# Gathering split around the first down products, columns ahead of weights, the eleventh place one matrix later

## The reference, cut to what matters

```
def run_block(args):
    xb, e = args
    hid = jax.nn.silu(xb @ w_gate[e]) * (xb @ w_up[e])
    return hid @ w_down[e]

ys = lax.map(run_block, (xs, blk_expert)).reshape(n_slots, D)
out = jnp.zeros((T + 1, D), jnp.float32).at[slot_tok].add(
    ys.astype(jnp.float32) * slot_gate[:, None])[:T]
```

## Time and profile before

| what | value |
|---|---|
| median of 3 runs | 941.4 us (941.03 to 943.34) |
| profiled execution, own time | 941.0 us |
| its span | 938.9 us |
| TensorE busy | 908.8 us, 97% |
| bytes moved by DMA | 286.12 MB, mean 305 GB/s |

### The profile page before, as it was taken

How to read it: one execution, slowest core, us unless ns; L and a number is a source line. 1 busy time by engine, 2 the same in 40 slices (tenths; PEclk the granted TensorE clock), 3 DMA queues, 4 the chain that set the end, 5 groups by cost and what they waited for, 6 DMA issues and landing times.

```text
span 938.9 us, 13252 instructions
## 1 busy us (share of the span) xinstructions
PE 908.8 (97%) x5218; PEld 537.0 (57%) x5218; DVE 277.9 (30%) x738; ACT 209.6 (22%) x500; POOL 198.7 (21%) x329
## 2 busy tenths in 40 slices
PE   7999999999999999999988999999999999999996
PEld 5788687544434444344433434488756558688544
DVE  2499824310101101011001011234135346250334
ACT  3365624211101111001101001132215511011640
POOL 0188400111111111111101111031003202013221
PEclk9999999999999999999999999999999999999999
DMA  9999975899999999999999999993300942202001
GB/s 349 428 425 419 405 297 203 347 384 431 428 427 429 427 428 424 429 427 428 428 427 429 427 422 425 427 414 140 156 2 19 427 171 114 89 14 77 1 1 45
DMA packets 24682, 286.12 MB, mean 305 GB/s; under 512 B 2738, under 2 KB 3506, under 8 KB 5426
## 3 DMA queue, kind: packets, MB, share of 16 engines
q1 hardware_dynamic: 23904, 283.99, 72.9%
q10 hardware_dynamic: 722, 1.33, 0.4%
HBM read 284.26 MB, written 1.05 MB: 304 GB/s over the span
## 4 chain that ended last, share of the span: by engine, by line
PE 74%; DMA 16%; DVE 6%; SPq 2%; issue 1%; POOL 0%; ACT 0%; POOLq 0%; DVEq 0%
PE bank L1032 18%; PE bank L1296 17%; DMA arena<-in_w_expert_up 10%; PE bank L1313 8%; PE bank L1517 5%; DVE bank L1772 5%; PE bank L1323 4%; DMA arena<-in_w_expert_down 3%; PE bank L1464 3%; DMA arena<-in_w_ada 3%; PE bank L1496 2%; PE bank L1284 2%; PE bank L1530 1%; PE bank L1655 1%; PE bank L1481 1%; PE bank L1044 1%
## 5 line engine op out<-in xcount | busy, mean ns | idle before, releaser
L1296 PE MATMUL bank<-arena 128*64 128x512 f32 x1024 | 226.2, 593 | 11.0 <-DMA arena<-in_w_expert_up 10.8
L1032 PE MATMUL bank<-arena 128*128 128x256 f32 (+1 forms) x992 | 211.1, 373 | 0.6 <-ACT arena L883 0.4
L1032 PEld LDWEIGHTS bank<-arena 128*128 128x128 f32 x992 | 183.2, 190 | 26.7 <-issue 3.0
L1296 PEld LDWEIGHTS bank<-arena 128*64 128x64 f32 x1024 | 75.8, 137 | 155.9 <-issue 154.8
L1313 PE MATMUL bank<-arena 128*64 128x512 f32 x512 | 116.9, 598 | 0.8 <-DVE arena L1963 0.6
L853 ACT ACTIVATE arena<-bank 128x512 f32<-128x512 f32 x32 | 19.1, 598 | 375.6 <-PE bank L1305 375.6
L1967 DVE TENSOR_TENSOR arena<-bank,arena 64x512 f32<-64x512 f32 x32 | 21.8, 683 | 263.5 <-ACT arena L849 263.5
L608 POOL COPY der<-arena 128x4 f32 (+1 forms) x30 | 5.6, 188 | 317.9 <-PE bank L1305 298.3
L1313 PEld LDWEIGHTS bank<-arena 128*64 128x64 f32 x512 | 33.9, 136 | 66.8 <-issue 64.7
L1323 PE MATMUL bank<-arena 64*128 64x256 f32 x512 | 65.8, 386 | 0.6 <-DVE arena L1985 0.5
L1772 DVE SCALAR_TENSOR_TENSOR bank<-arena,par,bank 128x256 f32<-128x256 f32 x143 | 58.3, 482 | 0.6
(11 more groups left out here) (262 smaller groups left out, 847.5 us busy)
## 6 DMA issues: line engine op xcount, KB each, us to landing
arena<-in_w_expert_down SPq DMA_DIRECT2D x29, 2048.0 KB, 30.7
arena<-in_w_expert_up SPq DMA_DIRECT2D x28, 2048.0 KB, 26.6
arena<-in_w_expert_gate SPq DMA_DIRECT2D x27, 2048.0 KB, 28.3
arena<-in_w_ada SPq DMA_DIRECT2D x8, 2048.0 KB, 39.3
arena<-in_w_expert_gate SPq DMA_DIRECT2D x10, 1024.0 KB, 31.5
arena<-in_w_ada SPq DMA_DIRECT2D x8, 1024.0 KB, 17.2
arena<-in_w_expert_up SPq DMA_DIRECT2D x8, 1024.0 KB, 34.3
arena<-in_w_kv SPq DMA_DIRECT2D x4, 2048.0 KB, 10.2
```

The source lines that it names most:

```text
L1032: mm = pe.matmul(bank[part:part + m, at:at + n], w[:, k, lo:lo + m], rhs[:, k0 + k, :], start=(i == 0), stop=(i == tiles - 1))
L1296: mm = pe.matmul(GU_BANK[half * WIN:(half + 1) * WIN, :], xw[b][:, k, :], w[:, k, :], start=(k == 0), stop=(k == KD - 1), skip_group_check ...
```

## The change

Three edits in one. The second half of the gathering is cut in two: four tiles come before the first down products and four behind them; the bank table of that half leaves out bank 1, which the down products fill. GpSimd copies the columns of an expert before it builds its weights, with a signal of its own for them (`columns_ready`); `begin` waits for the columns, and the turn waits for the weights. And the eleventh place takes the matrix with index 15 where it took 14.

```
-EXTRA, JOIN = RING, 14
+EXTRA, JOIN = RING, 15
...
-                plan(("gather", half, j), (7, 1, 2, 4, 5, 6, 7, 1)[j] if half else 1 + (j + 5) % 7)
+                plan(("gather", half, j), (7, 2, 4, 5, 6, 7, 2, 4)[j] if half else 1 + (j + 5) % 7)
...
                 at = pool.value_load(table[0:1, bass.ds(place, 1)], min_val=0, max_val=SLOTS_A)
+                if r == 0:
+                    pool.tensor_copy(xw[b], xg[:, :, bass.ds(at, WIN)]).then_inc(sem("columns_ready"), 1)
                 for t in range(NT):
-                    pool.tensor_scalar(weighted[b][:, t, :], rc[:, R_IOTA2:R_IOTA2 + P], own[:, b, t:t + 1],
+                    ins = pool.tensor_scalar(weighted[b][:, t, :], rc[:, R_IOTA2:R_IOTA2 + P], own[:, b, t:t + 1],
                                              own[:, b, NT + t:NT + t + 1], ALU.is_equal, ALU.mult)
-                pool.tensor_copy(xw[b], xg[:, :, bass.ds(at, WIN)]).then_inc(ready, 1)
+                if r:
+                    ins = pool.tensor_copy(xw[b], xg[:, :, bass.ds(at, WIN)])
+                ins.then_inc(ready, 1)
...
-            def turn(b):
+            def turn(b, e=None):
+                if e is not None:
+                    pe.wait_ge(win_ready, e + 1)
...
                 if not first:
-                    pe.wait_ge(win_ready, e + 1)
+                    if e > 1:
+                        pe.wait_ge(sem("columns_ready"), e - 1)
                     pe.wait_ge(hid_ready, e)
...
+            begin(0, 0, first=True)
+            gather(0)
+            begin(1, 1)
+            pe.wait_ge(sem("bank3_read"), BEFORE_EXPERTS[3])
+            turn(0, 0).then_inc(t_full, 1)
+            gather(1, range(KD // 2))
+            pe.wait_ge(sem("bank1_read"), BEFORE_EXPERTS[1])
+            finish(1, 1, second=True)
+            gather(1, range(KD // 2, KD))
+            begin(2, 0)
+            for b in range(4, 8):
+                pe.wait_ge(sem(f"bank{b}_read"), BEFORE_EXPERTS[b])
+            finish(2, 0, third=True)
```

More of the change, by code:

```diff
@@ L1276, in _, with gather @@
                 mm.then_inc(full(name), 1)
-            def gather(half):
-                for j in range(KD):
+            def gather(half, js=range(KD)):
+                for j in js:
                     name = ("gather", half, j)
@@ L1350, in begin @@
                 if e == EXPERTS - 1:
-                    turn((b - 1) % BODY).then_inc(t_full, 1)
+                    turn((b - 1) % BODY, e - 1).then_inc(t_full, 1)
                     pe.wait_ge(y_moved, e - 1)
@@ L1364, in finish @@
                         pe.wait_ge(hid_ready, e)
-                        turn(b1).then_inc(t_full, 1)
+                        turn(b1, e - 1).then_inc(t_full, 1)
                         pe.wait_ge(y_moved, e - 1)
@@ L1973, in _ @@
             gated(hid_ready)
[L1974 to L1977, removed]
+            for j in range(1, KD, 2):
+                gathered(0, j)
+            dve.wait_ge(silu_done, 2)
+            gated(hid_ready)
+            for j in range(1, KD, 2):
+                gathered(1, j)
+            dve.wait_ge(y_full, 1)
+            move_result(y_moved)
+            with dve.Fori(2, EXPERTS) as e:
                 dve.wait_ge(silu_done, e + 1)
```

## The result

| | before | after |
|---|---|---|
| median of 9 runs | 941.4 us | 944.26 us (942.6 to 945.49) |
| ratio | | 1.0028, 95% interval 1.002 to 1.0037 |
| profiled execution, own time and span | 941.0 and 938.9 us | 942.84 and 940.4 us |

The forecast was 942.9 us, in a range of 940.8 to 944.4. The changed kernel is slower by 2.6 us (the ratio), where 1.5 were forecast; its median lies in the range by 0.14 us; its profiled execution, the second fastest of the nine, is slower by 1.8, and its span by 1.5.

The account below looks back on a forecast made before the run. The prediction took TensorE to bound the kernel until 443 us and the load stream after. Profiled 941.0 plus 1.5 for the late stream gave 942.5; the median's 0.4 above the profiled run made 942.9 us, range 940.8 to 944.4.

Parts of the forecast that it names:

- What bounds the kernel: TensorE until 443 us, then the load stream: 14.7 us per expert against 13.0, setting the end at the last down matrix.
- steps 1 and 2: Before expert 2: gather ends 3.57 us later, earlier columns save 1.57, so expert 2 begins 2.0 to 2.1 us later.
- step 3: Experts after expert 2: the earlier columns are worth nothing, and weights come at most 0.61 us later.
- steps 4 and 5: SyncE's load issues: fifteenth matrix unchanged, sixteenth 0.75 us earlier, all later ones 2.07 us later with expert 2.
- Does the stream run dry: Loads issued at 218.27 us: the thin stock of 2.4 us swallows only part; stream 1.1 to 1.8 us late.
- The term for the late stream: Delay of the load stream near 219 us, passed on to the end: 1.5 us added to 941.0.
- the case with the main chance: Load stream late by 1 to 2.5 us, giving 942.4 to 943.9 us; chance 0.58.
- The absorbing one: At the 216.20 us issue, 2.4 us of loads in hand cover the 2.07 us delay: 941.4 to 942.0; chance 0.22.
- the gain: Sixteenth load issued earlier, between 196.00 and 216.20 us, gives up to 0.75 us: 940.7; chance 0.07.
- The clock rival: TensorE's clock falls behind the 2.80 us wait before expert 2, costing 3.6 to 7.1 us: 946.5 to 950; chance 0.07.
- the prediction's own signs of being wrong: Expert 2 by 196, no dip, clock under 1.00 at 198 to 206, or last down matrix not matching the dip's loss.
- the last rival: GpSimd's columns come no earlier, expert 2 begins at 199.65: 944.5 us; chance 0.06 together with the worst setup gap.

Follow-up runs that it names:

- pure delay: The kernel before with five or ten products of constants ahead of expert 2, nothing of the change: 943.83 us, ratio 1.0022, and 944.81 us, ratio 1.0041.
- early window: The changed kernel with the window of expert 2 copied on GpSimd as soon as the first half is gathered: 941.19 us, ratio 0.9994.

## Why the prediction was right, point by point

- **What bounds the kernel.** Right in the main: the chain passes to the stream at the same place, and every experiment that made expert 2 later made the end later, with dips of the stream in the profile after. The detail is off: the last down matrix is no longer waited for. In the two further profiles of the changed kernel the last wait of TensorE for a load that the profile shows comes at 549.23 and 548.01 us, where the prediction lets the stream set the end up to 597.2. TensorE and the stream are nearly level there.
- **Order and window, steps 1 and 2.** Forecast 198.08 to 198.15, measured 198.16, and in part by luck: this execution was 0.24 us earlier at 180 us, and the steps from there took 0.32 us more than the 13.54 forecast. The gap 2.80, measured 2.90. The setup of the column copy cost 1.02 us behind the ranks, as the weights' had (0.97), so taking nothing for it was right. On the common origin the delay is 2.3 us, not 2.07.
- **Later experts, step 3.** Right: worth nothing, by the kernel that has only this.
- **Eleventh place and issues, steps 4 and 5.** Right to 0.1 us as read; on the common origin the issues behind expert 2 come 0.2 us later than forecast.
- **Does the stream run dry.** Forecast 1.1 to 1.8 us late, measured 1.5 by the windows and 1.7 on the common origin. The trace's 1.55 us from issue to speed served; with the 0.6 us to the first byte in DMA: Bandwidth & Descriptors (Specifications) of the Trainium skill the loss would have been 0.2 us (the prediction's estimate from that page). In the profile after, the pair issued at 218.28 flows from 220.1 by this count, though 0.9 us of work was in hand.
- **The sum.** The term for the late stream was too small for the timed runs: 1.5 us against 2.6, and 3.6 and 3.1 in the two further timings. That 944.26 lies in the range is luck by a little: the case with the main chance, 942.4 to 943.9, did not come out, and the further medians are 944.66 and 944.67. The pure delay loses 2.1 us where this working would give it 1.5, so a good part of what is missing belongs to the delay itself: I let a stock of 2.4 us, read from one execution, swallow too much. The spans narrow the rest. Their means are 941.8, 942.1 and 941.9 us for the changed kernel against 939.2 to 939.6 for the kernel before, so 2.3 to 2.7 us lie in the span, where the pure delay has 2.2. Another 0.3 to 0.7 us lie outside it: own time less span is 2.4 to 2.9 us on average for the changed kernel and 2.1 to 2.2 for the kernel before and the pure delays. It is also 2.8 for the kernel with the columns alone and 2.7 with the early window, whose times are not longer, so I can't assign it. What is left in the span is open: the clock fell over the gap in one profile of three, with 1.4 us, but filling the gap gave no clear gain.
- **Rivals.** The absorbing one and the gain fell. The clock rival, given 0.07, is a real event in some executions, and a granted clock under 1.00 behind 198 us was one of the prediction's own signs of being wrong; it is absent from the profile after and present in two of the four with the gap of 2.90 us. Its price was forecast at 3.6 us and is 1.4 to 1.7 us of products, 1.0 us at the end. The time of the last rival (the columns are no earlier), 944.5 us, is nearer to the measured one than the forecast, but the trace rules it out: the columns are copied at 197.50, ahead of the weights, and expert 2 begins at 198.16 and not at 199.65.

## What to carry to other kernels

Where a stream of loads and a compute engine take turns as the bound, count bytes asked for less bytes moved at each issue: the thinnest stock tells where a delay of the engine becomes a delay of the end. Here a stock of 2.4 us was no cover for delays of 2.2 to 4.4 us: in the profiles it swallowed between nothing and 0.8 us of them. A single timing can flatter a forecast: one median here lay inside the range and two just above it. And when work is moved ahead of a hand-over, follow what is now last before the next step: here half a gather moved behind the down products put a copy on GpSimd, with its 2.9 us of latency, bare on the path.

## What the runs showed of the hardware that was not expected

TensorE's granted clock fell for a few microseconds at different places in different executions, of one program too. It fell behind waits of 4.37 and 3.03 us (one profile each), behind 2.90 us in two profiles of four, and behind three of the seven waits of 2.00 to 2.21 us for an up matrix; but also at the modulation products near 153 us behind a wait of 0.57 us, and once at 16 us behind 1.63 us. A wait of 2.01 us had the fall and one of 2.21 us had not, so in these profiles the length of the wait alone does not decide. All waits of 1.4 to 1.8 us per expert from 456 us on kept 1.00. TensorE: Matmul & The Clock Gate (Why this matters for your kernels) of the Trainium skill warns of idle gaps between matmul bursts; the falls behind 2.90 and 4.37 us agree with that, and the one at 153 us is not covered by it. Each fall cost 1.4 to 2.8 us of products.
